# Seven-product units in the first three down stages of a fused two-block kernel, with accumulating transfers and the residual kept in DRAM meanwhile

## The reference

```python
h = rms_norm(x, norm_ffn_pre[l])
f = (jax.nn.silu(h @ w_ffn_gate[l]) * (h @ w_ffn_up[l])) @ w_ffn_down[l]
x = x + rms_norm(f, norm_ffn_post[l])
```

## Time and profile before

| | |
|---|---|
| median of 3 runs | 2287.12 us (2287.00 to 2287.56) |
| the profiled execution | 2287.35 us, its span 2285.4 us, so that 1.95 us lie around the span |
| TensorE busy | 2274.2 us in 10681 matmuls |
| DVE busy | 1571.0 us |
| ACT busy | 1208.2 us |
| POOL busy | 25.5 us |
| TensorE clock granted | 1.000 of full speed |

### The profile page before, as it was taken

How to read it: one execution, slowest core, us unless ns; L and a number is a source line. 1 busy time by engine, 2 the same in 40 slices (tenths; PEclk the granted TensorE clock), 3 DMA queues, 4 the chain that set the end, 5 groups by cost and what they waited for, 6 DMA issues and landing times.

```text
span 2285.4 us, 27693 instructions
## 1 busy us (share of the span) xinstructions
PE 2274.2 (100%) x10681; PEld 1904.7 (83%) x10681; DVE 1571.0 (69%) x2058; ACT 1208.2 (53%) x1576; POOL 25.5 (1%) x35
## 2 busy tenths in 40 slices
PE   9999999999999999999999999999999999999998
PEld 7888888888888888888888888888888888888887
DVE  6677777756666668886677676675668755676864
ACT  6555655444445755554554454565555446556443
POOL 0000000000000000000000000000000000000000
PEclk9999999999999999999999999999999999999999
DMA  8566665766667556566666566756565665656564
GB/s 298 176 196 196 196 190 167 226 203 203 193 206 271 174 173 233 188 212 227 203 205 210 177 206 225 254 168 193 167 180 164 220 211 149 200 157 189 172 197 136
DMA packets 258578, 452.03 MB, mean 198 GB/s; under 512 B 23600, under 2 KB 63536, under 8 KB 257808
## 3 DMA queue, kind: packets, MB, share of 16 engines
q1 hardware_dynamic: 258016, 449.74, 62.2%
q10 hardware_dynamic: 432, 0.53, 0.1%
HBM read 434.99 MB, written 2.10 MB: 191 GB/s over the span
## 4 chain that ended last, share of the span: by engine, by line
PE 94%; DVE 4%; ACT 1%; issue 1%; DMA 0%; SPq 0%; DVEq 0%; ACTq 0%
PE pm L1086 28%; PE pm L1088 28%; PE pm L1087 28%; PE pb L730 1%; DVE wl L2430 1%; DVE raw L2438 1%; PE pb L912 1%; DVE wl L2444 1%; PE pb L810 1%; PE pb L1007 1%; PE pb L1009 0%; PE pb L1008 0%; PE pm L1007 0%; PE pm L1008 0%; PE pm L1009 0%
## 5 line engine op out<-in xcount | busy, mean ns | idle before, releaser
L2444 DVE TENSOR_TENSOR wl<-raw,wh 128x1024 fp32r<-128x1024 f32 (+2 forms) x746 | 897.4, 1209 | 580.1 <-ACT wh L1622 576.7
L1622 ACT ACTIVATE wh<-raw 128x1024 fp32r<-128x1024 f32 (+2 forms) x746 | 775.7, 1045 | 793.9 <-PE pm L1088 749.2
L1086 PE MATMUL pm<-wh,hTh 128*128 128x512 f32 x702 | 275.1, 392 | 0.8 <-DVE wl L2444 0.8
L1087 PE MATMUL pm<-wl,hTh 128*128 128x512 f32 x702 | 273.3, 389 | 0.0
L1088 PE MATMUL pm<-wh,hTl 128*128 128x512 f32 x702 | 273.3, 389 | 0.0
L1086 PE MATMUL pm<-wh,xT3h 128*128 128x512 f32 (+1 forms) x640 | 249.1, 389 | 0.0
L1088 PE MATMUL pm<-wh,xT3l 128*128 128x512 f32 (+1 forms) x640 | 244.6, 382 | 0.0
L1087 PE MATMUL pm<-wl,xT3h 128*128 128x512 f32 (+1 forms) x640 | 244.4, 382 | 0.0
L1087 PE MATMUL pm<-wl,x2Th 128*128 128x512 f32 x544 | 211.6, 389 | 0.0
L1086 PE MATMUL pm<-wh,x2Th 128*128 128x512 f32 x544 | 211.6, 389 | 0.0
L1088 PE MATMUL pm<-wh,x2Tl 128*128 128x512 f32 x544 | 211.6, 389 | 0.0
(11 more groups left out here) (469 smaller groups left out, 3704.8 us busy)
## 6 DMA issues: line engine op xcount, KB each, us to landing
raw<-in_w_in SPq DMA_DIRECT2D x286, 512.0 KB, 3.7
raw<-in_w_ffn_gate SPq DMA_DIRECT2D x88, 512.0 KB, 4.4
raw<-in_w_ffn_up SPq DMA_DIRECT2D x88, 512.0 KB, 5.8
raw<-in_w_ffn_down SPq DMA_DIRECT2D x88, 512.0 KB, 4.2
raw<-in_w_o SPq DMA_DIRECT2D x64, 512.0 KB, 4.3
raw<-in_w_in SPq DMA_DIRECT2D x68, 256.0 KB, 3.3
raw<-in_w_branch_b SPq DMA_DIRECT2D x32, 512.0 KB, 3.7
raw<-in_w_out SPq DMA_DIRECT2D x32, 512.0 KB, 4.6
```

Source lines behind the costliest of these rows:

```text
L1086: e.matmul(o, ah[:, kk, t], h[:, c], start=first and not begun, stop=False)
L1087: e.matmul(o, ah[:, kk, t], l[:, c], start=False, stop=False)
L1622: e.activation(h[:, 0:n], r[:, 0:n], ACT.Copy).then_inc(s["hi"], 1)
L2444: e.tensor_tensor(l[:, 0:n], r[:, 0:n], h[:, 0:n].bitcast(F32), ALU.subtract).then_inc(s["lo"], 1)
```

## The change

1. In down(0), down(1) and down(2) the first four weight rows of `d{q}0` and `d{q}1` go to a unit `ds{q}0`, those of `d{q}2` and `d{q}3` to a unit `ds{q}2`. The four groups of such a stage have 8 plain steps each, in place of 12. down(3) stays plain.
2. The token sums of a down stage are formed from `fT` in the middle of gate_up: `forms(1..3)` after `fg4`, `fg7` and `fg10`, into buffers `crows`, `craw`, `sform1`, and the sums of the unit `ds{q}0` into `CD`. All these lie where the first half of the residual `X` is. So `X` is written to a DRAM tensor `kept` in four transfers, one behind each of the `across` of c = 0 to 3, and read back in four after `ds22`. `forms(n)` for n of 1 or more waits until all four have landed (`d_kept` at 64).
3. The results of down(0) are put into `facc` by DVE's `joined` itself; those of down(1) and down(2) are joined in the buffers `CD` and `C11` to `C22` and added to `facc` by accumulating transfers that POOL issues (one of 1 MB and four of 256 KB per stage, semaphore `d_fa`). ACT's copies of line 1587 and DVE's adds of line 2400 for d1 and d2 are gone.
4. In the existing units, the join of the up group's second half comes 7 steps after the group, and no longer at once; the next unit's `b22` waits for the first half alone. In `fs9` the copy of `b11` is due at step 14 in place of 2 and waits for `d_fa` at 80, and its `gathered` comes 4 steps later.

```diff
+            if part < 3 and c % 2 == 0:
+                seven(f"ds{part}{c}", f"fT{part % 2}", (f"d{part}{c}", f"d{part}{c + 1}"),
+                      [rows[:, 512 * i:512 * i + 512] for i in (c, c + 1)], part + 1)
+            add(f"d{part}{c}", f"fT{part % 2}", rows, 512 * c, kts=range(4 if part < 3 else 0, 4 * n), ev=("d", 2))
...
         for c in range(11):
             yield from across(m.squares[2], "d_f", p.end[f"fu{c}"] + CARRIED, [("f_t", c + 1), ("f_l", 2 * c)], m.fcross)
+            if c < 4:
+                w.wait_ge(s["xr"], 8)
+                e.dma_start(kept[:, :, part(c)], m.X[:, :, part(c)]).then_inc(s["d_kept"], 16)
...
+        for c in range(4):
+            yield p.end["ds22"] + 2 + 3 * c
+            w.wait_ge(s["mm"], p.end["ds22"])
+            w.wait_ge(s["d_fa"], 96)
+            w.wait_ge(s["d_kept"], 64)
+            e.dma_start(m.X[:, :, part(c)], kept[:, :, part(c)]).then_inc(s["d_back"], 16)
...
     inverse_root("r0")
+    for q in (1, 2):
+        for c in (0, 2):
+            name = f"d{q}{c + 1}"
+            w.wait_ge(s["ev_d"], p.evac[name])
+            if q == 2:
+                w.wait_ge(s["d_fa"], 16 if c == 0 else 80)
+            if c == 0:
+                e.dma_start(m.facc[:, :, 0:1024], m.CD[:, :, :, :].rearrange("p h i n -> p h (i n)"), accum_op=ALU.add
+                            ).then_inc(s["d_fa"], 16)
+            else:
+                for i, C in enumerate(m.CG):
+                    e.dma_start(m.facc[:, i // 2, part(2 + i % 2)], C[:, :], accum_op=ALU.add).then_inc(s["d_fa"], 16)
...
+    def first_taken(name):
+
+        yield p.first[name] + (LATER if name == "fs9" else 2)
+        w.wait_ge(s["mm"], p.first[name] + 1)
...
+        elif name == "fs9":
+            w.wait_ge(s["d_fa"], 80)
+        e.activation(m.gather(name)[0], m.pb[4][:, :], ACT.Copy).then_inc(s["q_c"], 1)
...
+    def forms(n, at0):
+
+        (h, l), R, S = (m.fT[(n - 1) % 2], m.crows, m.craw) if n else (m.x2T, m.srows, m.sraw)
+        yield at0
+        if n:
+            w.wait_ge(s["f_l"], 2 * PARTS[n - 1][0] + 2)
+            w.wait_ge(s["d_kept"], 64)
+            if n == 3:
+                w.wait_ge(s["d_fa"], 16)
...
+    def gathered(name):
+
+        u, (C11, C12, C21, C22) = p.unit[name], m.gather(name)
+        yield p.end[name] + (2 if name[0] == "d" else GATHERED + 4 if name == "fs9" else GATHERED)
...
                 if c:
-                    yield from gathered(c)
-                    yield from joined(f"fg{c}", (m.C11, m.C21), 4 * c)
-                    yield from joined(f"fu{c}", (m.C12, m.C22), 4 * c)
+                    yield from gathered(f"fs{c}")
+                    yield p.end[f"fg{c}"]
+                    joined(f"fs{c}", 0, 0)
+                    joined(f"fs{c}", 0, 1)
+                    if c in SHAPED:
+                        yield from forms(SHAPED.index(c) + 1, p.end[f"fg{c}"] + 3)
+                    yield p.end[f"fu{c}"]
+                    joined(f"fs{c}", 1, 0)
...
+        for c in range(4):
+            name = f"d3{c}"
+            yield from memory_low(0, c)
+            yield p.end[name]
+            acc = banks(name)
+            w.wait_ge(s["mm"], p.end[name])
+            w.wait_ge(s["d_fa"], 160)
```

More of the change, by code:

```diff
@@ L93, in __init__ @@
         self.n = sum(w for _, w in cols)
-        self.pair = None
+        self.pair = self.joins = self.forms = None
 def weight_groups(a):
@@ L121, in weight_groups, with seven @@
     add("mv0", "memT", a["w_mv_2"][0], 0, gain="mem0", ev=("a", 2))
-    def seven(name, act, w_a, w_b, c0, kts):
-        out.append(Group(name, act, [(w_a[:, c0:c0 + 512], 512)], kts, ev=None))
-        out[-1].pair = [[(w[:, c0:c0 + 512], 512)] for w in (w_a, w_b)]
+    def seven(name, act, joins, blocks, forms):
+        out.append(Group(name, act, [(blocks[0], 512)], range(4), ev=None))
+        out[-1].pair, out[-1].joins, out[-1].forms = [[(w, 512)] for w in blocks], joins, forms
     def gate_up(part):
@@ L465, in buffers, with gather @@
     m.gcol = gcol
+    def gather(name):
+        if name[:2] == "ds" and name[-1] == "0":
+            return [m.CD[:, h, i, :] for h in range(2) for i in range(2)]
+        return [C[:, :] for C in m.CG]
+    m.gather = gather
     return m
@@ L522, in ready, with sync_program @@
     return "y_l", 5 * layer + (r // 2 + 1 if r < 5 else 4 + ln)
-def sync_program(nc, s, m, a, cst, cpool, gains, out, p):
+def sync_program(nc, s, m, a, cst, cpool, gains, out, kept, p):
     e = nc.sync
@@ L1017, in tensor_program @@
     n = 0
+    firsts, seconds = ([g.joins[i] for g in p.groups if g.pair] for i in range(2))
     for g in p.groups:
@@ L1084, in tensor_program @@
                     o = acc[:, half, 0:g.n]
-                    begun = joined and (half == 0 or g.name[:2] == "fg")
-                    e.matmul(o, ah[:, kk, t], h[:, c], start=first and not begun, stop=False)
+                    e.matmul(o, ah[:, kk, t], h[:, c], start=first and half >= joined, stop=False)
                     e.matmul(o, ah[:, kk, t], l[:, c], start=False, stop=False)
@@ L1580, in background @@
                     taken(0, f"fg{c}", m.FST[c % 2], ACT.Silu, "r0")
-            if q == 1:
-                for c in range(4):
-                    yield p.end[f"d0{c}"]
-                    acc = m.pm[p.acc[f"d0{c}"]]
-                    w.wait_ge(s["mm"], p.end[f"d0{c}"])
-                    w.wait_ge(s["xr"], 8)
-                    e.activation(m.facc[:, :, part(c)], acc[:, :, :], ACT.Copy).then_inc(s["ev_a"], 1)
+                if c in SHAPED:
+                    yield from forms_high(SHAPED.index(c) + 1, p.end[f"fg{c}"] + 8)
+            if q:
+                yield from first_taken(f"ds{q - 1}0")
+                yield from first_taken(f"ds{q - 1}2")
         for c in range(4):
@@ L1772, in joined @@
-    def joined(name, halves, value):
-        yield p.end[name]
-        w.wait_ge(s["mm"], p.end[name])
-        w.wait_ge(s["q_d"], value)
-        for half, C in enumerate(halves):
-            e.tensor_tensor(C[:, :], C[:, :], banks(name)[:, half, :], ALU.add).then_inc(s["ev_d"], 1)
+        yield at0 + 4
+        w.wait_ge(s["s_h"], n + 1)
+        hi, lo = m.sform[n > 0]
+        e.tensor_tensor(lo[:, :, :, :], S[:, :, :, :], hi[:, :, :, :].bitcast(F32), ALU.subtract).then_inc(s["s_l"], 1)
@@ new lines, in joined, with down @@
+    def joined(unit, i, half, into=None):
+        name, C = p.g[unit].joins[i], m.gather(unit)[2 * half + i]
+        w.wait_ge(s["mm"], p.end[name])
+        w.wait_ge(s["q_d"], 4 * p.unit[unit] + 4)
+        e.tensor_tensor(C if into is None else into, C, banks(name)[:, half, :], ALU.add).then_inc(s["ev_d"], 1)
+    def down(q):
+        for c in (0, 2):
+            unit = f"ds{q}{c}"
+            yield from gathered(unit)
+            for i in range(2):
+                yield p.end[f"d{q}{c + i}"]
+                for half in range(2):
+                    joined(unit, i, half, m.facc[:, half, part(c + i)] if q == 0 else None)
@@ L2459, in build @@
         p = Plan(weight_groups(a))
-        sync_program(nc, s, m, a, cst, cpool, gains, out, p)
+        kept = nc.dram_tensor("kept", (128, 2, DM), F32, kind="Internal").ap()
+        sync_program(nc, s, m, a, cst, cpool, gains, out, kept, p)
         gpsimd_program(nc, s, m, p)
```

161 lines of the change are left out of this document (82 added, 79 removed).

## The result

The changed kernel takes **2294.95 us** (median of 5 runs, 2294.32 to 2299.17) against 2287.47 for the kernel before (2287.00 to 2287.88) on the same chip: ratio 1.0039, 95% interval 1.0028 to 1.005. It is slower by more than the 0.2% that a measurement can tell. The profiled execution took 2294.66 us with a span of 2292.5, 7.1 us longer than before.

The account below looks back on a forecast made before the run. TensorE bounds the kernel, so only removed matmuls or closed gaps save time. Change -8.16 - 2.85 + 10.9 = -0.1 us against the profiled 2287.35 gives 2287.25, 0.23 above the median: forecast 2287.0 us, range 2279.5 to 2294.5.

Parts of the forecast that it names:

- the pauses of the kernel before: In the ten existing units: 98.08 us against 95.2 for their matmuls, put at 2.85 us more.
- three places that I had at nothing: Waits on accumulating transfers and other added DMA traffic, in fs9, at d3 and elsewhere: put at 0.
- the queue behind the first form: DVE's work from the split at 998.80 to the sixth product's split at fs5: put at 18.3 us.
- the matmuls and the units: Six new units save 36 matmuls, 8.16 us; all units together run 10.9 us over 9.52 each.
- The central wait: DVE at forms(1) waits for the fourth kept store, landing taken as 4.5 us; fs5 loses 7.15 us.
- Transfers otherwise: Added DMA traffic and accumulating transfers, 6.8 us for 1 MB, 9.2 for four, are covered: 0 us.
- Rival 2: Accumulating transfers come late, ACT in fs9 or DVE at d30 waits; at 22 us each, 2295; chance 0.18.
- Its condition, 18 us: At fs9 or d30: lateness costs time once the four transfers need more than about 18 us from the join.
- Rival 3: DVE can't carry the down stages; five ds units give back 6.6 us more, 2293.6 us; chance 0.13.
- Rival 1: kept has landed when DVE reaches forms(1), so fs5 costs 0.8 us: 2280.7 us; chance 0.14.
- The rule weighed: GpSimd's transfer descriptors are not written while DVE holds their shared port, so accumulating transfers would come late; forecast cost nothing.

Follow-up runs that it names:

- e2: Changed kernel with the last pair of down(2) added to facc by four VectorE sums, not accumulating transfers: 2290.80 us.
- e3: Changed kernel with the 1 MB load of norm_ffn_post moved earlier, behind the across of c = 6: 2294.27 us.
- e6: Changed kernel with the first pair of down(2) (1 MB) summed on VectorE, the last pair left to GpSimd: 2298.69 us.
- e8: Changed kernel with accum_op struck out, so transfers overwrite facc, and each GpSimd group waiting for the one before to land: 2289.73 us.
- e10: Changed kernel with the joins of ds20 cut from 512 to 64 columns, output incomplete: 2301.62 us.
- e11: Changed kernel with the residual's return moved behind d31: 2294.30 us.
- e14: Changed kernel with ds20's joins on 64 of 512 columns, down(2)'s accumulating megabyte held until three steps behind ds22, return behind d31: 2293.88 us.
- e1: Changed kernel with the kept stores early, two behind each of the first two across: 2290.33 us.
- e7: Changed kernel with store and gain early and all sums into facc on VectorE, no accumulating transfers: 2288.46 us.
- e13: Changed kernel with store and gain early, last pair on VectorE, down(2)'s megabyte held until three steps behind ds22, return behind d31: 2282.03 us.

## Why the prediction was wrong

I said 2287.0 us; it was 2294.95, 0.45 above the range. From the start of fs1 to the end of down(3) the profiled execution is 6.8 us longer than before. The fewer matmuls and the pauses of the kernel before give -8.16 - 2.88, the units +10.6, and three places that I had at nothing +6.5; together +6.1. Of the other 0.7 us, 0.6 lie in distances under 0.3 us, too short for the table; 0.4 us more of the span lie ahead of fs1, where nothing was changed. (The sums of the forecast hold but for two roundings: 98.08 - 95.2 is 2.88 and not 2.85, and the queue behind the first form adds up to 18.2 and not 18.3.)

- **Right: the matmuls and the units.** 10645 matmuls, 8.16 us less. The pauses in and ahead of the units were put at 10.9 us and come to 10.6: fs5 6.7 (7.15 forecast), fs8 0.98 (0.8), ds20 0.99 (0.8), three `ds{q}2` 0.92 (1.2). fs2 is off, 0.65 in place of 0.08, and this made up for fs5 and the `ds` units, which came short: that the sum fits to 0.3 is partly luck. The profiles of e2, e3, e6, e8, e10, e11 and e14, whose code is the same up to there, show no pause at fs2, so it belongs to this one execution. The central wait was in its place, of 6.22 us, with the store's landing at 3.7 us where I had taken 4.5. e1 shows the price: 5.8 us of pauses.
- **Wrong: "Transfers otherwise", put at 0.** This step failed: these transfers cost 3.8 us at d30, 2.3 at S2 and 0.45 behind ds12, 6.5 in all. It took the landing time of a plain load, 6.8 us for 1 MB and 2.3 each for the four, and asked only whether somebody waits for `facc`. Three things were missing. An added byte takes the DMA engines twice as long (e8). The four transfers do not follow at their issue rate: GpSimd stood 2.66 and 6.11 us behind the first of each four, until that one had landed, and they were complete after 15.0 and 16.6 us where I had 9.2. And they run into X's return and the weights: 389 GB/s, a DMA share of 1.05 from 1450 to 1470 us. Price at d30: 3.8 us of pauses (all gone in e2, and in e8 with the addition struck out); how much of it is the traffic's stays open (1.5 by e11, nothing by e14).
- **Wrong in the same step: what the megabyte does to others.** S2 behind ds22 loses 2.3 us. VectorE sits at 25.83 of 26 us before it (1412 to 1438), so that its last splits free the buffers late and SyncE issues S2's weights at 1437.35; with the megabyte issued at 1433.28 under way their landing takes 8.4 us (4.4 in e14, where it is held). Neither alone cures it: with the transfer gone and its sums on VectorE, S2 stays late (e6, e7), with VectorE relieved the transfer moves ahead of the crossings (e10), and as a plain copy it still stands in front of them (e8). Holding it back does, beside the other edits of e13 and e14.
- **The rivals.** Rival 2 was the right one, at half of its size and at d30 alone; ScalarE's copy in fs9 shows no wait. Its condition, 18 us, was too far off: the wait ended 16.7 us behind GpSimd's first issue (1483.08 - 1466.38) and cost 3.8, so the point lies near 13, an estimate from this one execution. My 18 counted the three slabs ahead, 8.2 us, in full, but of VectorE's 6.88 us only 3.1 were covered: splits stand on VectorE behind the waiting sum. Rival 3 was wrong as the cause of the time, but e6 and e7 show how near it was. Rival 1 is what e1 made: 5.8 us less, where I had 6.35.
- **The rule weighed.** I took it for the support of rival 2. In e8 the megabyte is issued at 1432.58 us while VectorE has no gap from 1427.35 to 1436.5, and it lands in 4.9 us. So this transfer was not starved of descriptors by a busy VectorE, as the Trainium skill, SBUF — State Buffer, SBUF: two separate sides, would have it for a VectorE that holds the shared port; whether these forms of its instructions do, no run here shows. At d30, where the transfers came late, the wait is gone when the addition is (e8).
- **Open.** Why GpSimd's issues have gaps behind the first accumulating transfer (2.66, 6.11, in e6 9.16 us) and not behind a plain one. The kernel has no wait between the four. What the traces show is where the gaps end. The first ones of the changed kernel's two fours, issued at 1316.20 and 1466.38, have these times to landing:

```profile
DMA to landing us min/median/max: 3.3/3.3/3.3
...
DMA to landing us min/median/max: 6.7/6.7/6.7
```

They land at 1319.51 and 1473.13, and the second ones are issued at 1319.77 and 1473.39, each time 0.26 us later. It is so in all twelve profiles with accumulating transfers, in 20 gaps: each ends 0.20 to 0.26 us after the landing of an earlier transfer of the four. So whatever makes a first one land later delays the other three by as much.

## What to carry to other kernels

A transfer that accumulates is not a free sum: cost it at twice its bytes in the busiest stretch that it meets, reckon that the ones behind the first are issued only when it has landed, and ask what small urgent transfers stand behind it, not only who waits for its result. It pays where VectorE is full and nobody needs the sum or its buffers soon (in down(1), by e7: the next user, ScalarE's copy in fs9, comes 18.7 us after the first issue and does not wait), and not for the last pair in front of a reader (e2). And a store that a later wait needs belongs as early in its queue as its data allow: moving it brought no new pause at fs1 to fs4 and gave 5.8 us of pauses back.

## What the runs showed of the hardware

- **Accumulation doubles a packet.** In the trace the 4096-byte packets of the accumulating megabytes take 0.403 us on average (512 of them), plain ones from the same queue 0.175 (1024, e8), and plain ones from SyncE's queue 0.177 in the changed kernel.
- **Big and urgent transfers collide across queues.** The megabyte is issued by GpSimd, the crossings by SyncE, and still 2 us in their order decide over 6.43 or 0.83 us of waiting. A plain megabyte does it too: issued 0.7 us sooner in e8, it goes with a wait of 3.72 us.
- **A pause can halve the clock.** In e3 two starts of TensorE were 4.7 us apart at d30; then the granted clock was 0.50, that is 1.2 GHz, for 6 us, with 14 matmuls where 27 belong. Windows of e3:

```profile
1483.00:1488.00 5.00, 0.67 (x4) 0.93 0.37 92
1488.00:1494.00 6.00, 6.00 (x14) 0.50 0.58 174
1494.00:1500.00 6.00, 6.00 (x27) 0.99 0.88 308
```

So the pause cost 4.5 us, and of the 7.46 us at that place the other 3 are the clock's. In the changed kernel's profiled execution, where no two starts were more than 2.4 us apart, the clock stayed at 1.00; but in e2 two starts 2.3 us apart at S2 were followed by seven matmuls at the lower clock. What decides it, no run tells.
